# A two-model block with its residual kept turned, and every large product 256 columns wide

## What is computed

```
a1   h += 0.5 * swiglu(rms_norm(h)) @ wo        (each FFN: 1024 -> 2 x 2816 -> 1024)
gla  h += [gated linear attention, pooling](rms_norm(h)) @ w_out
a2   h += 0.5 * FFN        b1  h += 0.5 * FFN
dsa  h += sparse attention(rms_norm(h)) @ w_out  (top-64 keys by an index score)
b2   h += 0.5 * FFN        then h = rms_norm(h) * final_norm, the input of the second model
c1   h += 0.5 * FFN
mla  h += (two attentions, gated)(rms_norm(h)) @ w_o
c2   h += 0.5 * FFN, the output
```

## Time and profile before

| | |
|---|---|
| median of 3 runs | 1446.95 us (1446.36 to 1446.98) |
| the profiled run | 1446.5 us, its span 1444.7 us |
| instructions | 18750 |
| PE busy | 1439.0 us (100%), 7822 products |
| PEld busy | 1237.5 us (86%) |
| DVE busy | 1009.8 us (70%) |
| ACT busy | 777.7 us (54%) |
| POOL busy | 92.9 us (6%) |
| DMA | 266.83 MB, mean 185 GB/s |

### The profile page before, as it was taken

The page is one execution under the profiler, slowest core; times in us unless marked ns, Lnnn a source line. Parts: engine busy times, 40 slices in busy tenths (PEclk is TensorE's granted clock), DMA queues, the critical chain, the costliest instruction groups (busy, mean ns, idle before and its releaser), DMA issues.

```text
span 1444.7 us, 18750 instructions
## 1 busy us (share of the span) xinstructions
PE 1439.0 (100%) x7822; PEld 1237.5 (86%) x7822; DVE 1009.8 (70%) x1333; ACT 777.7 (54%) x971; POOL 92.9 (6%) x117
## 2 busy tenths in 40 slices
PE   9999999999999999999999999999999999999999
PEld 7888888888888888888888888888888888888887
DVE  6886466787755877459878764787646987787753
ACT  6654355655534655445656543565436876465532
POOL 0000003000000000006100000000000820000000
PEclk9999999999999999999999999999999999999999
DMA  9855563456555556545455556575556543556552
GB/s 332 279 180 184 161 206 117 156 194 199 185 184 193 197 189 194 190 139 171 150 198 196 187 178 208 157 226 183 189 176 217 190 146 118 174 193 210 182 189 73
DMA packets 205621, 266.83 MB, mean 185 GB/s; under 512 B 6944, under 2 KB 148880, under 8 KB 205280
## 3 DMA queue, kind: packets, MB, share of 16 engines
q1 hardware_dynamic: 204320, 261.23, 54.9%
q0 software_dynamic: 1072, 4.35, 0.8%
q10 hardware_dynamic: 144, 0.05, 0.0%
HBM read 264.56 MB, written 1.05 MB: 184 GB/s over the span
## 4 chain that ended last, share of the span: by engine, by line
PE 93%; DVE 3%; ACT 2%; DMA 1%; issue 0%; SPq 0%; DVEq 0%
PE ps L667 32%; PE ps L674 16%; PE ps L599 14%; PE ps L601 14%; PE ps L600 13%; PE ps L652 1%; DMA raw<-in_ffn_wi 1%; PE ps L872 1%; DVE wlo L1695 1%; PE ps L777 1%; PE ps L810 1%; DVE wlo L1699 1%; ACT whi L1252 0%; DVE d_i L2092 0%; DVE d_m L2088 0%
## 5 line engine op out<-in xcount | busy, mean ns | idle before, releaser
L1252 ACT CAST whi<-raw 128x2048 fp32r<-128x2048 f32 (+5 forms) x275 | 474.7, 1731 | 221.1 <-PE ps L601 217.4
L667 PE MATMUL ps<-xt,whi 128*128 128x512 f32 x2112 | 502.3, 391 | 0.3 <-ACT whi L1252 0.3
L667 PEld LDWEIGHTS ps<-xt,whi 128*128 128x128 f32 x2112 | 388.8, 188 | 78.0 <-DVE xt L2290 0.8
L1699 DVE TENSOR_TENSOR wlo<-raw,whi 128x2048 fp32r<-128x2048 f32 (+5 forms) x131 | 264.5, 2024 | 192.9 <-ACT whi L1252 192.8
L1695 DVE TENSOR_TENSOR wlo<-raw,whi 128x128 fp32r<-128x128 f32 (+6 forms) x265 | 311.8, 1218 | 65.6 <-ACT whi L1252 65.5
L674 PEld LDWEIGHTS ps<-xt,wlo 128*128 128x128 f32 x2112 | 254.9, 188 | 8.2
L674 PE MATMUL ps<-xt,wlo 128*128 128x256 f32 x2112 | 256.6, 276 | 0.0
L599 PE MATMUL ps<-whi,xt 128*128 128x512 f32 (+4 forms) x304 | 112.6, 370 | 0.4 <-ACT m_fk L1383 0.4
L601 PE MATMUL ps<-whi,xt 128*128 128x512 f32 (+4 forms) x304 | 109.7, 361 | 0.0
L600 PE MATMUL ps<-wlo,xt 128*128 128x512 f32 (+4 forms) x304 | 109.5, 360 | 0.0
L599 PEld LDWEIGHTS ps<-whi,xt 128*128 128x128 f32 x304 | 57.3, 189 | 9.7 <-ACT m_fk L1383 0.6
(11 more groups left out here) (423 smaller groups left out, 1950.2 us busy)
## 6 DMA issues: line engine op xcount, KB each, us to landing
raw<-in_ffn_wi SPq DMA_DIRECT2D x85, 1024.0 KB, 4.9
raw<-in_ffn_wo SPq DMA_DIRECT2D x40, 1024.0 KB, 5.0
raw<-in_ffn_w_gate SPq DMA_DIRECT2D x22, 1024.0 KB, 5.1
raw<-in_ffn_w_up SPq DMA_DIRECT2D x22, 1024.0 KB, 5.1
raw<-in_ffn_w_down SPq DMA_DIRECT2D x20, 1024.0 KB, 4.9
raw<-in_w_in SPq DMA_DIRECT2D x14, 1024.0 KB, 5.2
raw<-in_even_w_in SPq DMA_DIRECT2D x6, 1024.0 KB, 5.4
raw<-in_ffn_wo SPq DMA_DIRECT2D x8, 512.0 KB, 3.7
```

Of the source, the lines that this page charges most:

```text
L667: return e.matmul(Pair(job.name).ap[:, b, :], whi[:, v % SPLIT, 256 * j + 128 * b:256 * j + 128 * b + 128], XS[:, j, :, :].rearrange("p h ...
L1252: e.copy(whi[0:n, v % SPLIT, c], raw[0:n, v % RAW, c]).then_inc(s_hi.mark(*[(v, j) for j in js]), 1)
L1699: e.tensor_tensor(low_slot(v)[0:n, c], raw[0:n, v % RAW, c], whi[0:n, v % SPLIT, c].bitcast(F32), ALU.subtract).then_inc(s_lo.mark(*[(v, j ...
```

## The change

The residual X is kept turned throughout: 128 partitions (features), 8 feature tiles, 256 tokens. The x input that was loaded turned for the first norm is the residual; its second load, with tokens on the partitions, goes. The output leaves turned and is rearranged on the host, as the input is. Down and output products are made by `across`, which holds a block of the weights and moves 256 columns of activations, so that the result comes out turned. `turn_x` on TensorE, the copies and adds of the two PSUM halves and `scale_turn` are gone: gate and up products move x hi and x lo in two products of 256 columns into the same place, gate in bank 0 and up in bank 1 of one pair. `x_high` and `x_low` split X straight from SBUF. The sum of squares over the features is now a sum over partitions: ScalarE squares two feature tiles at a time, VectorE adds them up (`add_squares`), and TensorE multiplies by ones, into a row for all partitions (`sum_row`, FFNs) or a column (`sum_column`, attention stages). The reciprocal root of a row runs on 128 x 256 (`rsqrt_row`). `add_to_x` takes a multiply and an add where the row scale is to be applied. The final norm between the two models is applied to X in c1 (`final_scale`, `final_x`). High and low weights of the turned products lie 16 words past their slot's start in even tiles, 48 in odd ones.

```diff
-WIDE_AT = 16
+WIDE_AT = (16, 48)
...
+        def high_slot(v):
+            at = WIDE_AT[v % 2] if plan[v][0] in turned_jobs else 0
+            return whi[:, v % SPLIT, at:at + 2048]
...
-            q.wait_ge(*s_dve[("xt", "in"), 7])
-            e.dma_start(X[:, :, :], T["x"][0].rearrange("(t p) d -> p t d", p=128)).then_inc(s_x.mark("x"), 16)
             load(4)
...
+            def across(job, i, j0=0, j1=4):
...
+                def three(j, m, stop):
+                    kt, c = k0 // 128 + j + job.k_off, slice(512 * j + 128 * m, 512 * j + 128 * m + 128)
...
+                    e.matmul(o, high_slot(v)[:, c], job.act.hi[:, kt, :], start=i == 0 and j == 0 and (very_last or m % 2 == 0), stop=False)
+                    e.matmul(o, high_slot(v)[:, c], job.act.lo[:, kt, :], start=False, stop=False)
+                    return e.matmul(o, low_slot(v)[:, c], job.act.hi[:, kt, :], start=False, stop=stop)
...
+            def sum_row(x):
+                pair = take(("rs", x))
+                q.wait_ge(*s_pool["ones_row"])
+                q.wait_ge(*s_dve["sum", x])
+                t = e.matmul(pair.ap[:, 0, 0:256], ones_row[:, :], SQ[:, 0, :], start=True, stop=True)
+                if x == "b2":
+                    t = e.matmul(pair.ap[:, 1, 0:256], ones_row[:, :], SQF[:, 0, :], start=True, stop=True)
+                t.then_inc(s_turn.mark(("rs", x)), 1)
+                give(("rs", x), s_dve["rsb", x])
...
                 def high(job, j, b, stop):
...
-                    return e.matmul(Pair(job.name).ap[:, b, :], whi[:, v % SPLIT, 256 * j + 128 * b:256 * j + 128 * b + 128],
-                                    XS[:, j, :, :].rearrange("p h t -> p (h t)"), start=j == 0, stop=stop)
+                    o, w = rows(job, b), high_slot(v)[:, 256 * j + 128 * b:256 * j + 128 * b + 128]
+                    e.matmul(o, w, XS[:, j, 0, :], start=j == 0 and b == 0, stop=False)
+                    return e.matmul(o, w, XS[:, j, 1, :], start=False, stop=stop)
...
                 wide(g[1], 0, 4)
                 wide(g[0], 4, 8)
-                give(g[0].name, s_dve["gsum", name, 0])
                 wide(u[0], 4, 8)
-                give(u[0].name, s_dve["usum", name, 0])
+                sum_row(f.x)
+                give(u[0].name, s_dve["h", name, 0])
                 wide(g[1], 4, 8)
...
-                steps(d[0], 0)
-                for i in range(1, 6):
-                    steps(d[0], i)
+                for i in range(6):
+                    across(d[0], i)
...
                 steps(ga, 0)
-                turn_x("a1", 1)
                 steps(gk, 0)
                 steps(ga, 1)
+                sum_column("a1")
                 steps(gk, 1)
```

ScalarE and VectorE in the first tiles of an FFN (first ScalarE, then VectorE):

```diff
                 else:
                     unit()
-                    turn_x(f.x, 1)
-                    squares(f.x, 1)
-                gate_taken(0)
-                unit()
-                if f is c1:
-                    squares("fin", 0)
-                    squares("fin", 1)
-                up_taken(0)
+                    x_high(f.x, 1)
+                    all_squares(f.x, 1)
+                unit()
                 unit()
                 if f is a1:
-                    squares("in", 0)
-                    squares("in", 1)
+                    for i in range(4):
+                        squares("in", i)
...
+                    x_low(f.x, 1)
+                    add_squares(f.x, 2, 3)
+                unit()
                 unit()
                 if f is a1:
+                    add_squares("in", 0, 1, 2, 3)
+                unit()
+                q.wait_ge(*s_turn["rs", f.x])
                 if f is c1:
+                    rsqrt_row(f, Pair(("rs", f.x)).ap[:, 0, 0:256], RFB[:, :])
+                else:
+                    rsqrt_row(f, Pair(("rs", f.x)).ap[:, 0, 0:256], f.RSB[:, :], ("rsb", f.x))
+                unit()
+                if f is c1:
+                    final_scale()
                 gate_scale(0)
...
+            def squares(x, i):
+                dst = SQ if i == 0 else junk[:, :].rearrange("p (b t) -> p b t", b=2)
...
+                if i > 1:
+                    q.wait_ge(*s_dve["added", x, i - 1])
+                q.wait_ge(*s_act.now())
+                e.activation(dst[:, :, :], X[:, 2 * i:2 * i + 2, :], ACT.Square).then_inc(s_act.mark(("sq", x, i)), 1)
...
+            def final_scale():
+                f, pair = c1, Pair(("rs", "b2"))
+                t = f.U[:, 0, 0, :]
...
+                e.tensor_tensor(t, pair.ap[:, 1, 0:256], RFB[:, :], ALU.mult).then_inc(s_dve.mark(), 1)
...
+                e.tensor_tensor(t, t, RFB[:, :], ALU.mult).then_inc(s_dve.mark(), 1)
+                rsqrt_row(f, t, f.RSB[:, :])
...
+                e.tensor_tensor(f.RSB[:, :], f.RSB[:, :], RFB[:, :], ALU.mult).then_inc(s_dve.mark(("rsb", "b2")), 1)
...
+            def last_add():
+                for m in range(4):
+                    q.wait_ge(*s_mm["last", m])
+                    t = c2.GS[:, m // 2, m % 2, :]
+                    e.tensor_tensor(t, pairs[m // 2].ap[:, m % 2, 0:256], c2.RSB[:, :], ALU.mult).then_inc(s_dve.mark(), 1)
                     after_mine()
+                    e.tensor_tensor(X[:, 4 + m, :], X[:, 4 + m, :], t, ALU.add).then_inc(s_dve.mark(("x", "c2", 4 + m)), 1)
...
                 unit()
-                turn_x("b1", 1)
-                unit()
+                x_low("b1", 1)
+                add_squares("b1", 2, 3)
+                unit()
+                row_scale("b1")
                 unit()
                 q.wait_ge(*s_act["di"])
```

More of the change, by code:

```diff
@@ L287, in program @@
             job.at[i] = v
+        turned_jobs = {job for f in (a1, a2, b1, b2, c1, c2) for job in f.g + f.u + f.d} | set(g_out + d_out + c_out)
+        def high_slot(v):
+            at = WIDE_AT[v % 2] if plan[v][0] in turned_jobs else 0
+            return whi[:, v % SPLIT, at:at + 2048]
         def low_slot(v):
[L291 to L321, removed]
+            at = WIDE_AT[v % 2] if plan[v][0] in turned_jobs else 0
+            return wlo[:, v % SPLIT, at:at + 2048]
         def pieces(v):
@@ L560, in sync @@
                 load(v)
[L561 to L568, removed]
+            for k in range(8):
+                q.wait_ge(*(s_dve["x", "c2", k] if k >= 4 else s_dve["x", "c2", 0, k // 2]))
+                e.dma_start(out[:, 256 * k:256 * k + 256], X[:, k, :]).then_inc(s_out.mark(("x", k)), 16)
+            q.wait_ge(*s_out["x", 7])
         def tensor(e):
@@ new lines, in add_squares @@
+            def add_squares(x, *blocks):
+                for i in blocks:
+                    last = i == 3
+                    for name, total in ((x, SQ),) + ((("fin", SQF),) if x == "b2" else ()):
+                        q.wait_ge(*s_act["sq", name, i])
+                        after_mine()
+                        if i:
+                            part = final_squared(i) if name == "fin" else junk[:, :].rearrange("p (b t) -> p b t", b=2)
+                            e.tensor_tensor(total[:, :, :], total[:, :, :], part, ALU.add).then_inc(s_dve.mark(("added", name, i)), 1)
+                if 3 in blocks:
+                    for name, total in ((x, SQ),) + ((("fin", SQF),) if x == "b2" else ()):
+                        after_mine()
+                        e.tensor_tensor(total[:, 0, :], total[:, 0, :], total[:, 1, :], ALU.add).then_inc(
+                            s_dve.mark(*([("sum", x)] if name == "fin" or x != "b2" else [])), 1)
@@ L1894, in all_gains, with final_x @@
+            def final_x():
+                q.wait_ge(*s_act[("xh", "b2"), 7])
+                q.wait_ge(*s_act["sq", "fin", 3])
+                for k in range(8):
+                    e.scalar_tensor_tensor(X[:, k, :], X[:, k, :], gain("fin", k), RFB[:, :], ALU.mult, ALU.mult).then_inc(
+                        s_dve.mark(*([("x", "fin")] if k == 7 else [])), 1)
+                after_mine()
             def all_gains():
```

516 lines of the change are left out of this document (219 added, 297 removed).

## The result

The changed kernel takes 1457.17 us (median of 4 runs, 1456.09 to 1458.07), the kernel before 1446.97 beside it (4 runs, 1446.36 to 1447.09): a ratio of 1.0072, 95% interval 1.006 to 1.0085. It is slower by 0.7%, as forecast (1455, range 1443 to 1489); most terms of the sum and the places of the two largest waits held. One place was wrong (dsa), one wait was missed (gla), and the clock's part in c1 had no term.

A forecast was written before the change was run, and what follows sets the result against it. TensorE, busy over the whole span, was taken as the bound. 17.2 us off, 6.3 of products with ones and waits in a1, c1, dsa, mla and the tail summed to +7.7 us: 1455 us, range with rivals 1443 to 1489.

The forecast's parts named there:

- the offset's term: Weights of gate, up, down and output products at 16 and 48 words: 0 us taken, bounds 0 and 67.
- the rival's 1488: Odd tiles, weights at 48 words, read badly: 5040 products cost 6.6 ns more, 1488 us; chance 0.22.
- Off TensorE, -17.2: Work leaving TensorE: residual transposes 13.9 us, row-scale turns 1.3 us, switches between product forms 2 us; 17.2 us off.
- Products with ones, +6.3: Nine sums of squares by plain fp32 products with ones on TensorE: 6.3 us added, bounds 3 and 8.
- The wait in a1, 8.9 and 2.5: First stage: TensorE waits 8.9 us for the sum of squares behind u[0]; lower clock afterwards costs 2.5 us.
- The wait in c1, 2.7: In c1, g[3] waits for its PSUM pair until VectorE finishes `final_scale`: 2.7 us, bounds 0 and 6.
- The wait in dsa, 2.9: In dsa, TensorE waits at the index turn for VectorE's rotations: 2.9 us, bounds 0 and 4.
- gla, "has slack": In gla, the same reckoning as for dsa's wait finds slack; no time put in the sum.
- mla 0.5, tail 1.1: Wait in mla 0.5 us, bounds 0 and 2; last output pieces ready later after the last product, 1.1 us.
- The rival that the first stage does not wait: Between u[0] and g[1], the squares are there in time: 11.4 us less, 1443.5 us; chance 0.16.
- The rival of queues that grow behind waits: ScalarE's casts in c1 and mla come late in turn: 1465 us; chance 0.07.
- The fixed part for each product: Each halving of a product costs up to 1.6 ns: 6 us more, 1461 us; chance 0.05.

The follow-up runs named there:

- e6: The changed kernel with the weights of even and odd tiles both at offset 0 instead of 16 and 48 words: 1517.06 us.
- e10: The changed kernel with the weights of even and odd tiles both at offset 48 words instead of 16 and 48: 1496.28 us.
- e11: The changed kernel with the weights of alternating tiles at offsets 16 and 32 words instead of 16 and 48: 1480.47 us.
- e7: The changed kernel with the weights of even and odd tiles both at offset 16 words instead of 16 and 48: 1472.61 us.
- e1: The changed kernel with a1's products with ones (`sum_row`) moved behind tile 3, the second up product: 1447.53 us, ratio to the kernel before 1.0003.
- e9: The changed kernel with repairs in a1, c1, gla and dsa together, including earlier low parts on VectorE in a1 and c1: 1439.90 us, ratio to before 0.9955.
- e4: The changed kernel with the products with ones in gla and dsa two steps earlier, in the middle of their block: 1454.76 us.
- e5: The changed kernel with gla's and dsa's products with ones two steps earlier and dsa's index turn one step later: 1453.09 us.
- e2: The changed kernel with the PSUM pair of b2's sums in c1 handed back behind its last reader: 1455.41 us.
- e3: The changed kernel with b2's PSUM pair in c1 handed back earlier and ScalarE's cast of u[3] ahead of silu(0): 1454.62 us.

## Why the prediction was right

- *The products.* 10080 of 256 columns, 113 to 114 ns in odd and even tiles, but for 6% at 118 (2.7 us in all): the 0 of the offset's term nearly held (e6 shows that the 67 at its other end was real). The reason given, that 48 words is the same kind of offset as 16, did not: e10 shows 48 words slow by themselves, and e11 that another neighbour of 16 is slow. Another pair of offsets would have brought the rival's 1488 into reach (e7, e11, e10: 1473, 1480, 1496). The number held, its reason did not.
- *Off TensorE, -17.2.* The transposes gave -15.2, as reckoned; the switches and halvings lie in the -1.2 of the FFNs for a predicted -2, with the slower spacing behind four of the sums by ones in it (0.3 each).
- *Products with ones, +6.3.* 3.0 us of issue for the rows, 0.4 for each of three columns, and 0.3 of slower products behind each of five rows: about 5.9. The size was near and the parts were not: a row was priced at 0.73 us, 0.18 of it lost on entry and exit, and in the trace it costs its 0.43 and less than 0.01 more on both sides; the rest comes in the 72 products behind it, which no row before could show.
- *The wait in a1, 8.9 and 2.5.* The cast at 21.70 (21.5 predicted), the last add at 29.33, TensorE released at 29.90 after 8.97 us idle. a1's lost time was 10.5 more than before, for 11.4. Moving the call (e1) gave 8.1 of it back and e9 all. This step decides the sign.
- *The wait in c1, 2.7.* 2.2, on g[3]'s pair, released by `final_scale`. No term stood for the clock behind it, about 1.7 us in this profile; with some slower products the place cost 4.4.
- *The wait in dsa, 2.9.* The size was short and the place wrong. The table has 5.3: 1.8 for the wait shown below, 1.7 for the lower clock behind it, 0.6 for a later wait on VectorE (L931), 0.4 for the column sum (which has its own term) and 0.7 for products at the slower spacing. The sum put the low part of dq0's first block behind the row's factors and ahead of the rotations, and asked only when the rotation is done. But TensorE wants that low part itself, and stood idle for 1.84 us until it came at 665.12. The timeline of VectorE and TensorE:

```profile
660.34 0.16 DVE L1704 TENSOR_SCALAR nv<-ps 128x2 f32<-128x2 f32 x1 [1.24 <-PE ps L661]
...
662.78 2.29 DVE L1640 TENSOR_TENSOR wlo<-raw,whi 128x2048 fp32r<-128x2048 f32 x1
...
665.12 0.50 PE L569 MATMUL ps<-whi,xt 128*128 128x512 f32 x1 [1.84 <-DVE wlo L1640]
```

VectorE idles 1.24 us for the products with ones, spends 2.4 us on thirteen small operations, and only then makes the low part; in the change the row's factors stand between TensorE and its weights, where before they needed no product and were ready at 649.2. The turn's wait exists too (e1, e4), and a step more of work hides it (e5).
- *gla, "has slack".* Wrong by 0.8: the same queue makes TensorE wait 0.8 us for a low part there (2.6 less the 1.8 of dsa). 0.4 of the table's 1.3 is the column sum.
- *mla 0.5, tail 1.1.* 0.3 and 0.9.

The sum was +7.7 for a measured +9.6 in the profiled runs (1446.50 and 1456.09). Of the table's regions dsa, c1 and gla are 5.4 more than their terms; a1, the products with ones, mla and the tail are 1.7 less; the FFNs' switches gave 0.8 less than the 2 put, and 0.3 lie outside the span. That would be 4.8 too much instead of 1.9: 2.9 of the products with ones stand in the regions and are counted twice here. The mechanism and the two largest waits were right; that the total came within 1.9 us is in part luck, since terms put too high made up for waits that were missed or too small.

The rival that the first stage does not wait was priced at 1443.5; e1, which takes most of that wait away (1.3 us are left), ran 1447.5: a1 kept 3.2 us of lost time, and the other waits were larger than put. The rival of queues that grow behind waits did not come: mla lost 0.3 more than before, and in c1 ScalarE's cast was late only once e2 let TensorE arrive earlier. The fixed part for each product did not either; the halves in the earlier trace rows had spoken against it, and 113.1 ns in the trace after settles it. One of the listed signs, a wait of 3 us before the index turn, was not in the profile. The Trainium skill (TensorE: Matmul & The Clock Gate, Back-to-back issue gap) has N/2.4 + 2.5 ns for a product by itself, which would be 109.2 ns for 256 columns, with 2.5 ns to be paid twice; here, in a stream of products with their own weight loads, the trace differs on both.

## What to carry to other kernels

When work moves off the engine that bounds the kernel onto others, list for each new result who waits for it and what that engine could do in the meantime: here the place of one call cost some 8 us of a loss of 10, and moving it cost nothing. For a queue that serves the bound engine twice (factors for later, weights for now), write down when each is wanted, not only when the last one is done. When a wait is removed, the next one behind it is often within a microsecond or two; reckon that one before the first is undone.

## What the runs showed of the hardware

- The same 256-column fp32r product with its own weight load has three spacings, 113.3, about 118 and 120.0 ns. The offsets of the weights of alternating tiles change how many products have which: 60 us between the best and the worst pair tried.
- A plain fp32 product of 256 columns among them (two in c1) is followed by a change of the spacing from 113.3 to 117.8 ns (five times in the change, twice in e7) or back (three times in e7). It takes 0.43 us by itself and less than 0.01 more on both sides.
- After 2.2 us of an idle TensorE the granted clock fell to the 1.2 GHz level for some 3.4 us in two profiles (the change, e5) and stayed at 2.4 GHz in two others (e1, e4): such a wait costs 2.2 us, or about 4. After 9 us idle in a1 (8.3 to 9.9) the lower level was there in all nine profiles that have that wait.
- A clock that drops ahead of another wait is free: dsa lost 8.7 and 8.6 us with it (the change, e3), 9.0 and 8.6 without (e1, e2).
